# Decode states with channels on partitions, and a new order at the start and at the mixer-to-FFN seam

## The chip, the cores and the metric

One Trainium2 chip, 8 NeuronCores, one program on all of them. Each core takes one prompt sequence (2048 tokens) and 16 decode streams of 4 tokens (64 tokens, "the decode tile", tile 16). The metric is the device time of the slowest core in microseconds. Engines: PE (TensorE, matmuls and transposes), DVE (VectorE), ACT (ScalarE), POOL (GpSimd; here small copies, products and the queue of the casting weight loads), SP (SyncE; here only the queue of all other transfers).

## What is computed

One layer of a hybrid decoder in f32, weights cast to bf16 for PE:

```python
mod = silu(c) @ w_ada + b_ada            # shift1, scale1, gate1, shift2, scale2, gate2
h   = rmsnorm(x, g_pre_mix) * (1 + sc1) + sh1
v_pool, x_conv, B, C = split(h @ w_in)   # 4 x 512 channels
y_A = pool_scale * groupwise(mean_window(v_pool) - v_pool)   # windows 2, 4, 8, 16
y_B = B * dwconv3(C * x_conv)
x   = x + gt1 * rmsnorm([y_A | y_B] @ w_out, g_post_mix)
h2  = rmsnorm(x, g_pre_ffn) * (1 + sc2) + sh2
a,b = split(dwconv3(h2 @ w_up))          # 2 x 2816 channels
x   = x + gt2 * rmsnorm((silu(a) * b) @ w_down, g_post_ffn)
```

The decode streams carry state into the windows: the last 15 rows of v_pool (`state_pool`), the last 2 rows of C * x_conv (`state_conv`) and of the up projection (`state_ffn`). The new states of decode and prompt are outputs beside both y.

## The kernel before

Tokens are cut into 16 tiles of 128 and the decode tile of 64; four tiles make a chunk (0 to 3). Inside the mixer and FFN data lie with channels on partitions and tokens along the row.

Start: SP loads `cT`, the identity, `vecs` and x tiles 0 to 3 into four slots (`XT`); POOL issues eight pieces of w_ada (scale1, shift1), then `w_in_p`, `pool_w` and four `w_in_j`. A tile is squared and summed on ACT (line 540), Sqrt on ACT (542), reciprocal and product on DVE (547, 585), then its slot is free; transposed by PE (`h_tr`, 298) and scaled on the way out of PSUM (`h_ev`, 687/689, ACT or DVE).

Mixer: 16 steps `n` (chunk c = n // 4, s = n % 4). A step has `P_item(c, s)`, the pool projection of group s into bank 5, evicted by ACT (809), windows on DVE; and `V_item(c, s)`, three projections into banks 2, 3, 4 (885 to 901). In chunk 1 (`samp`) each 512-column matmul of these has a 64-column one for the decode tile beside it, so `HS`, the transposed decode tile (`samp_tr_ev`), must be there before chunk 1. The decode tile is loaded at step 2 (lines 1028 to 1031) and needs a slot. Output tiles follow five steps later: `o_tile(t)` reloads x, multiplies by w_out into banks 0 and 1 and adds the normalised result to x (`post_b1`, 933 to 941); `b2(t)` normalises for the FFN. `gate_piece` (four for gate1 at n = 4) makes the gate rows on PE (736) and DVE (741, 742) and needs the `rows` tensor. w_out follows the last w_ada piece on POOL's queue.

States before: HBM holds them row-major. `state_in` loads them with rows on partitions into `STG0` to `STG2`, PE turns them with f32 transposes, ACT copies them into `VS` [128, 4, 16, 19] and `QS` [128, 4, 16, 6]. `state_out` turns them back (two groups of four transposes, two ACT copies, 20 transfers, one of them from HBM to HBM). `ffn_state_piece` brings `state_ffn` in by six loads and 44 transposes during pairs 6 to 16 of the first FFN group; `ffn_state_out` takes it out by 44 transposes, 11 ACT copies and 22 transfers among the last down projections.

Seam: after step 15 output tiles 16 and 11 to 15, `b2` of each, the four gate2 pieces, `state_out` and `h2_all(2)` are written ahead of the FFN. FFN: group 0 (chunks 0 and 1), its down projections of tiles 0 to 7, group 1 (chunks 2, 3 and the decode tile), down projections 8 to 16. A group has 22 pairs; a pair is two chunks of 16 matmuls into one of three bank pairs (`next_pair`), evicted by ACT (1217, 1218) and two DVE products (1220, 1224), Silu on ACT (1285), product on POOL (1234). `hook0(i)` puts `b2(15)`, `h2_T(3, ..)`, the w_down loads and the state pieces behind pair i.

Order: every operation is recorded with the regions it reads and writes. Then `Sched.arrange` (184 to 234) plays all of it through with fixed costs and writes one order per engine: at each step it takes the engine that can start first and, among what could start there within 0.25 us, the operation that stands first in the program. Engines then run in that order and wait for semaphores, whatever really comes first. Transfers have no such cost of their own but one shared bus:

```python
if o.dma:
    bus = max(bus, free[e] + 1.5) + o.nbytes * DMA_US_PER_BYTE
    o.fin = bus + 0.5
```

`x` tile loads of chunk 1 depend on a PE operation: tiles 4 and 5 on the last shift1 piece (`first_x`), tiles 6 and 7 on the first `P_item` (`firsts[0]`), state and rows loads on the second (`firsts[1]`).

Of the kernel before, what the change touches and what calls it, by code (L numbers as in the profile page):

```python
# [7 lines left out]
F32 = mybir.dt.float32  # L8
# [8 lines left out]
NS = 16  # L17
# [19 lines left out]
DMA_US_PER_BYTE = 1.0 / 380e3  # L37
# [81 lines left out]
class Sched:  # L119
# [64 lines left out]
    def arrange(self):  # L184
# [11 lines left out]
        bus = 0.0  # L196
# [13 lines left out]
        while todo:  # L210
# [90 lines left out]
def build_program():  # L301
# [11 lines left out]
    stp_d = din("st_pool", [NS * PB, 512])  # L313
    stc_d = din("st_conv", [NS * 2, 512])
    stf_d = din("st_ffn", [NS * 2, 2 * DFF])
# [12 lines left out]
    npp_d = dout("npp", [PB, 512])  # L328
    ncp_d = dout("ncp", [2, 512])
    nfp_d = dout("nfp", [2, 2 * DFF])  # L330
    nps_d = dout("nps", [NS, PB, 512])
    ncs_d = dout("ncs", [NS * 2, 512])
    nfs_d = dout("nfs", [NS * 2, 2 * DFF])
# [33 lines left out]
    IDF = alloc([128, 128], F32)  # L367
# [10 lines left out]
    TMP = alloc([128, D], F32)  # L378
    h2a_off = cur[0]
# [29 lines left out]
    SMPP = alloc([128, 4, TS + PB], F32)  # L409
    SMP2 = alloc([128, 4, 34], F32)  # L410
# [4 lines left out]
    XN1 = [alloc([128, D], BF16) for _ in range(4)]  # L415
    x_end = cur[0]
# [34 lines left out]
    STF = alloc([128, NCH, 34], F32)  # L451
# [7 lines left out]
    def new_sem(name):  # L459
# [13 lines left out]
    r_vecs, r_vd, r_sc, r_rep, r_id, r_idb, r_invc, r_eps = [R(n) for n in  # L473
                                                             ("vecs", "vd", "sc", "rep", "id", "idb", "invc", "eps")]
# [82 lines left out]
    dma1("sp", IDF, ident_d, writes=[r_id])  # L557
# [66 lines left out]
    K.op("dve", lambda e: e.tensor_copy(IDB, IDF), reads=[r_id], writes=[r_idb])  # L624
# [178 lines left out]
    def P_item(c, g, samp):  # L803
# [27 lines left out]
        if c < 3:  # L831
            K.op("pool", lambda e: e.tensor_copy(V[:, 1:16], V[:, 513:528]), reads=[], writes=[rV])
        else:
            K.op("pool", lambda e: e.tensor_copy(SMPP[:, g, TS:TS + PB], V[:, 513:528]), reads=[rV], writes=[r_smpt[g]])
        if samp:
# [4 lines left out]
            def f_ev(e):  # L840
                e.activation(out=v3[:, :, PB:PB + DS], in_=ps3.rearrange("p (s r) -> p s r", r=DS), func=AF.Copy)
                return e.activation(out=SMPP[:, g, 0:TS], in_=ps3, func=AF.Copy)
            K.op("act", f_ev, reads=[r_ps[sbank]], writes=[r_vs[g], r_smpp[g]])
# [40 lines left out]
    def V_item(c, j, samp):  # L884
# [17 lines left out]
        if c < 3:  # L902
            K.op("pool", lambda e: e.tensor_copy(Q[:, 0:2], Q[:, 512:514]), reads=[], writes=[rQ])
        else:
            K.op("pool", lambda e: e.tensor_copy(SMP2[:, j, 32:34], Q[:, 512:514]), reads=[rQ], writes=[r_smp2t[j]])
        if samp:
# [14 lines left out]
            K.op("pool", lambda e: e.tensor_copy(SMP2[:, j, 0:32].rearrange("p (s r) -> p s r", r=2), q3[:, :, 4:6]),  # L921
                 reads=[r_qs[j]], writes=[r_smp2[j]])
# [86 lines left out]
    for n in range(16):  # L1009
# [4 lines left out]
        if n == 10:  # L1014
            for rr in H2Areg:
                rr.alias(r_stg + [r_rows1])
            h2_all(0)
# [4 lines left out]
        if c < 3:  # L1022
# [5 lines left out]
            if n == 2:  # L1028
                h_load(16, deps=[firsts[1]])
                h_act(16)  # L1030
                h_dve(16)
        if c < 3 and s == (3 if c == 0 else 2):
            for gi in range(4):
                h_T(c + 1, gi, misc_bank(), "act" if gi < 3 else "dve")
            if c == 0:
                samp_tr_ev(misc_bank(), XN2[0], r_xn2[0], G1T, S1T, [r_g1, r_s1], HS, 0, r_hs)
# [8 lines left out]
        if n == 1:  # L1045
            rows1_in([firsts[1]])
            state_in([firsts[1]])
# [11 lines left out]
        if n == 9:  # L1059
# [6 lines left out]
           [r_xc, r_acc, r_xcs, r_accs] + r_dbs + r_db + r_vs + r_qs + r_smpp + r_smpt + r_smp2 + r_smp2t)  # L1066
# [14 lines left out]
    def state_out():  # L1081
        K.op("pe", tr_group([PS[0:TS + PB, 5, g * 128:(g + 1) * 128] for g in range(4)],
                            [SMPP[:, g, :] for g in range(4)], IDF), reads=r_smpp + r_smpt + [r_id], writes=[r_ps[5]])
        K.op("act", lambda e: e.activation(out=TT_[0][0:TS + PB, 0:512], in_=PS[0:TS + PB, 5, :], func=AF.Copy),
             reads=[r_ps[5]], writes=[r_tt[0]])
        K.op("pe", tr_group([PS[0:34, 5, j * 128:(j + 1) * 128] for j in range(4)],
                            [SMP2[:, j, :] for j in range(4)], IDF), reads=r_smp2 + r_smp2t + [r_id], writes=[r_ps[5]])
        K.op("act", lambda e: e.activation(out=TT_[1][0:34, 0:512], in_=PS[0:34, 5, :], func=AF.Copy),
             reads=[r_ps[5]], writes=[r_tt[1]])
        out_ops.append(K.dma("sp", lambda e: [e.dma_start(out=nps_d[s, PB - DS:PB, :], in_=TT_[0][s * DS:(s + 1) * DS, 0:512])  # L1090
                                              for s in range(NS)] + [e.dma_start(out=npp_d, in_=TT_[0][TS:TS + PB, 0:512])],
                             next_misc(), NS + 1, reads=[r_tt[0]]))
# [45 lines left out]
    STGF = USB[0].rearrange("p a b c -> p (a b c)")  # L1138
    STG_F = [STGF[:, 0:384], None]

# [7 lines left out]

    STA = TMP
    r_sta = r_tmp  # L1150
    s_sta = new_sem("sta")

    def ffn_state_piece(n, bank):
        q0, q1 = n * 8, min(NCH, n * 8 + 8)
        nq = q1 - q0
        dma1("sp", STA[0:32, 0:nq * 128], stf_d[:, q0 * 128:q1 * 128], writes=[r_sta], sem=s_sta)
        K.op("pe", tr_group([PS[:, bank, q * 32:(q + 1) * 32] for q in range(nq)],
                            [STA[0:32, q * 128:(q + 1) * 128] for q in range(nq)], IDF[0:32, 0:32]),
             reads=[r_sta, r_id], writes=[r_ps[bank]])
        K.op("act", lambda e: e.activation(  # L1160
# [272 lines left out]
```

How the kernel before makes its waits and increments, by code:

```python
    def emit(self, eng, e):  # L248
        waited = {}
        for o in self.ops[eng]:
            need = {}
            for d in o.deps:
                s, v = d.sig
                if need.get(s, 0) < v:
                    need[s] = v
            for s, v in need.items():
                if waited.get(s, 0) < v:
                    e.wait_ge(s.h, v)
                    waited[s] = v
            if o.fn is None:
                continue
            r = o.fn(e)
            if o.dma:
                assert len(r) == o.n, (len(r), o.n)
                for i in r:
                    i.then_inc(o.sem.h, 16)
            elif o.need:
                r.then_inc(o.sig[0].h, 1)
```

## Time and profile before

| | |
|---|---|
| median of 3 runs | 798.16 us (797.77 to 799.29) |
| profiled execution | 796.71 us, span of its slowest core 795.2 us |
| spans of the 8 cores | 788.0 to 795.2 us, clock 0.972 to 0.984 |
| PE busy | 717.5 us, 90% |
| DVE, ACT, POOL busy | 488.9, 337.4, 206.1 us |
| DMA packets | 27211, of them 4741 under 512 B |

The page is of the slowest core. Busy time is the sum of an engine's instructions in a stretch; a stretch in which PE's busy time equals its length is bound by PE. "Idle before" and the name behind the arrow say what released an instruction that had to wait.

### The profile page before, as it was taken

How to read it: one execution, taken by the hardware profiler on the slowest of the kernel's cores; microseconds unless marked ns; L12 is line 12 of the kernel's file. 1: busy time of each engine (PE TensorE's matmuls, PEld its weight loads, DVE VectorE, ACT ScalarE, POOL GpSimd, SP SyncE). 2: the span in 40 equal slices, each digit the busy share in tenths (PEclk: the TensorE clock that was granted, in tenths of full speed). 3: DMA queues.
4: the chain of work that ended last, by engine and by line, in shares of the span. 5: the costliest groups of instructions: out<-in, count | busy, mean ns of one | idle time of the engine just before them, and what ended most of it. 6: DMA issues, size and time to landing. Idle time of an engine off the chain costs nothing.

```text
span 795.2 us, 12501 instructions; the slowest of 8 cores (788.0 to 795.2 us)
## 1 busy us (share of the span) xinstructions
PE 717.5 (90%) x4204; PEld 351.4 (44%) x4204; DVE 488.9 (61%) x660; ACT 337.4 (42%) x607; POOL 206.1 (26%) x266
## 2 busy tenths in 40 slices
PE   0269498998999999999999999999999999999995
PEld 0224254444444554444444444444444444444442
DVE  1246278686687787777767732227888888832222
ACT  1226235644565466655444421114544445422221
POOL 4001010011010001543444420003667667530000
PEclk9979599999899999999999999999999999999999
DMA  8999977319942496488874523234344343003321
GB/s 152 200 191 218 200 186 187 106 54 193 214 150 93 115 239 201 80 166 155 152 141 80 79 54 131 104 110 108 56 83 75 63 85 67 1 13 139 116 78 40
DMA packets 27211, 96.88 MB, mean 122 GB/s; under 512 B 4741, under 2 KB 4997, under 8 KB 26236
## 3 DMA queue, kind: packets, MB, share of 16 engines
q0 software_dynamic: 11904, 47.85, 35.7%
q1 hardware_dynamic: 15244, 48.23, 18.3%
q8 instruction: 34, 0.56, 0.3%
q14 instruction: 29, 0.24, 0.1%
HBM read 125.61 MB, written 18.66 MB: 181 GB/s over the span
## 4 chain that ended last, share of the span: by engine, by line
PE 80%; DMA 11%; DVE 3%; ACT 3%; issue 2%; POOL 1%; DVEq 0%; another core or an unknown queue 0%; ACTq 0%; POOLq 0%; SPq 0%
PE ps L785 50%; PE ps L290 20%; PE ps L281 6%; DMA arena<-w_in_p 5%; DMA arena<-x 3%; DMA arena<-w_ada 2%; PE ps L298 2%; PE ps L736 1%; ACT arena L687 1%; DVE arena L935 1%; ACT arena L540 1%; POOL arena L521 1%; DVE arena L1220 0%; DVE arena L1224 0%; DVE arena L939 0%
## 5 line engine op out<-in xcount | busy, mean ns | idle before, releaser
L785 PE MATMUL ps<-arena 128*128 128x512 bf16 (+1 forms) x2400 | 442.6, 346 | 12.4 <-DMA arena<-w_in_p 6.1
L785 PEld LDWEIGHTS ps<-arena 128*128 128x128 bf16 x2400 | 201.9, 99 | 242.1 <-issue 24.5
L290 PE MATMUL ps<-arena 128*128 128x512 bf16 (+1 forms) x748 | 162.9, 379 | 0.0
L1220 DVE SCALAR_TENSOR_TENSOR arena<-ps,arena 128x1023 f32<-128x1023 f32 x88 | 112.7, 1281 | 53.8 <-ACT arena L1218 53.5
L1234 POOL TENSOR_TENSOR arena<-arena 128x1024 bf16<-128x1024 f32 x44 | 103.6, 2354 | 86.7 <-DVE arena L1224 61.5
L1224 DVE SCALAR_TENSOR_TENSOR arena<-ps,arena 128x1022 f32<-128x1022 f32 x88 | 112.8, 1281 | 9.2
L290 PEld LDWEIGHTS ps<-arena 128*128 128x128 bf16 (+1 forms) x748 | 73.6, 99 | 86.7 <-issue 0.4
L540 ACT ACTIVATE arena<-ps 128x1024 f32<-128x1024 f32 (+1 forms) x34 | 34.8, 1023 | 155.6 <-PE ps L290 128.5
L547 DVE RECIPROCAL arena<-arena 128x1 f32<-128x1 f32 (+1 forms) x68 | 10.8, 158 | 143.8 <-ACT arena L542 143.7
L1218 ACT ACTIVATE arena<-ps,arena 128x1024 f32<-128x1024 f32 x88 | 97.5, 1109 | 0.1
L1217 ACT ACTIVATE arena<-ps 128x2 f32<-128x2 f32 x88 | 15.1, 172 | 129.8 <-PE ps L785 117.3
L281 PE MATMUL ps<-arena 128*128 128x512 bf16 (+1 forms) x288 | 68.3, 385 | 0.7 <-DVE arena L935 0.7
L298 PE MATMUL ps<-arena 128*128 128x128 bf16 (+4 forms) x380 | 34.3, 242 | 37.1 <-DVE arena L721 19.3
L521 POOL DMA_DIRECT2D arena<-w_up x44 | 25.8, 585 | 144.8 <-PE ps L785 114.7
L540 ACT ACTIVATE arena<-arena 128x1024 bf16<-128x1024 f32 (+1 forms) x34 | 35.9, 1055 | 35.3 <-DMA arena<-x 31.3
L1285 ACT ACTIVATE arena<-arena 128x1024 f32<-128x1024 f32 x44 | 46.5, 1057 | 8.9 <-DVE arena L1228 8.8
L298 PEld LDWEIGHTS ps<-arena 128*128 128x128 bf16 (+4 forms) x380 | 28.7, 113 | 48.0 <-issue 43.6
L939 DVE TENSOR_TENSOR arena<-arena 128x1024 f32<-128x1024 f32 (+1 forms) x34 | 41.6, 1225 | 9.1 <-DMA arena<-x 4.6
L935 DVE SCALAR_TENSOR_TENSOR arena<-ps,arena 128x1024 f32<-128x1024 f32 (+1 forms) x34 | 43.6, 1283 | 5.5 <-DVE arena L547 2.9
L687 ACT ACTIVATE arena<-ps,arena 128x512 bf16<-128x512 bf16 x48 | 33.6, 780 | 22.2 <-PE ps L298 13.6
L281 PEld LDWEIGHTS ps<-arena 128*128 128x128 bf16 (+1 forms) x288 | 27.6, 99 | 33.7 <-issue 4.1
L821 DVE TENSOR_TENSOR arena<-arena 128x512 f32<-128x512 f32 (+6 forms) x40 | 27.7, 693 | 11.4 <-ACT arena L809 9.5
(89 smaller groups left out, 381.8 us busy)
## 6 DMA issues: line engine op xcount, KB each, us to landing
arena<-w_up POOLq DMA_DIRECT2D x44, 512.0 KB, 6.2
arena<-x SPq DMA_DIRECT2D x32, 512.0 KB, 8.0
y<-arena SPq DMA_DIRECT2D x32, 512.0 KB, 2.7
arena<-w_ada POOLq DMA_DIRECT2D x24, 512.0 KB, 16.1
arena<-y SPq DMA_DIRECT2D x16, 512.0 KB, 3.7
arena<-w_down POOLq DMA_DIRECT2D x3, 1536.0 KB, 15.2
arena<-w_in_j POOLq DMA_DIRECT2D x4, 768.0 KB, 54.6
arena<-rows SPq DMA_DIRECT2D x4, 512.0 KB, 15.8
```

Source lines behind the costliest of these rows:

```text
L281: inst = e.matmul(out_ap, lhs_list[i], rhs_list[i], start=(i == 0), stop=(i == n - 1))
L290: inst = e.matmul(out_ap, lhs_list[i], rhs_list[i], start=(first and i == 0), stop=(last and i == n - 1))
L298: inst = e.transpose(o, i, ident)
L540: K.op("act", lambda e: e.activation(out=junk, in_=src_ap, func=AF.Square, accum_out=STAT[0:rows, k_ss, t:t + 1]), reads=src_regs, writes= ...
L785: inst = e.matmul(o_, l_, r_, start=st, stop=sp_)
L935: K.op("dve", lambda e: e.scalar_tensor_tensor(TMP[0:rows, :], psv, STAT[0:rows, k_rs, t:t + 1], GTt[0:rows, :], ALU.mult, ALU.mult), read ...
L939: lambda e: e.tensor_tensor(XT[xi][0:rows, :], TMP[0:rows, :], XT[xi][0:rows, :], ALU.add),
L1218: return e.activation(out=tv, in_=psv, func=AF.Copy, scale=fw_of(2, c))
L1220: K.op("dve", lambda e: e.scalar_tensor_tensor(tv[:, 1:1024], psv[:, 0:1023], fw_of(1, c), tv[:, 1:1024], ALU.mult, ALU.add), reads=rp + [ ...
L1224: K.op("dve", lambda e: e.scalar_tensor_tensor(tv[:, 2:1024], psv[:, 0:1022], fw_of(0, c), tv[:, 2:1024], ALU.mult, ALU.add), reads=rp + [ ...
L1234: K.op("pool", lambda e: e.tensor_tensor(GT_[:, i, 0:1024], ta, tb, ALU.mult), reads=[rTa, rTb], writes=[r_g[i]])
L1285: K.op("act", lambda e, ta=ta: e.activation(out=ta, in_=ta, func=AF.Silu), reads=[rTa], writes=[rTa])
```

## The change

Host code now lays the states out as [128 partitions, channel block, stream, row] and pads the rows of the first two to 19 and 6. The kernel loads them straight into `VS`, `QS` and `STF`, and stores them straight from there; all state transposes, their staging tiles and ACT copies go.

```diff
-DMA_US_PER_BYTE = 1.0 / 380e3
+DMA_US_PER_BYTE = 1.0 / 340e3
@@ arrange
-                bus = max(bus, free[e] + 1.5) + o.nbytes * DMA_US_PER_BYTE
-                o.fin = bus + 0.5
+                move = o.nbytes * DMA_US_PER_BYTE
+                if e == "pool":
+                    bus = max(bus, free[e] + 1.5) + move
+                    o.fin = bus + 0.5
+                else:
+                    side = max(side, free[e] + 1.5) + 1.7 * move
+                    bus += move
+                    o.fin = side + 0.5
@@ start: the decode tile after tiles 0 to 3
+    h_load(16)
+    h_act(16)
+    h_dve(16)
...
+    samp_tr_ev(2, XN2[0], r_xn2[0], G1T, S1T, [r_g1, r_s1], HS, 0, r_hs)
@@ state_in
+        dma1("sp", VS.rearrange("p a b c -> p (a b c)"), stp_d, writes=r_vs, deps=deps)
+        dma1("sp", QS.rearrange("p a b c -> p (a b c)"), stc_d, writes=r_qs, deps=deps)
@@ P_item, V_item, chunk 3 (c == 3) and samp
-            K.op("pool", lambda e: e.tensor_copy(SMPP[:, g, TS:TS + PB], V[:, 513:528]), ...
+            out_ops.append(dma1("sp", npp_d[:, g, :], V[:, 513:528], reads=[rV]))
-                return e.activation(out=SMPP[:, g, 0:TS], in_=ps3, func=AF.Copy)
-            K.op("pool", lambda e: e.tensor_copy(SMP2[:, j, 32:34], Q[:, 512:514]), ...
+            out_ops.append(dma1("sp", ncp_d[:, j, :], Q[:, 512:514], reads=[rQ]))
-            K.op("pool", lambda e: e.tensor_copy(SMP2[:, j, 0:32]. ...
@@ steps
-            if n == 2:
-                h_load(16, deps=[firsts[1]])
-                h_act(16)
-                h_dve(16)
         if n == 1:
-            rows1_in([firsts[1]])
-            state_in([firsts[1]])
+            state_in([firsts[0]])
+        if n == 2:
+            rows1_in([firsts[2]])
@@ state_out
+        out_ops.append(K.dma("sp", lambda e: [e.dma_start(out=nps_d[:, g, :, :], in_=VS[:, g, :, DS:DS + PB]) for g in range(4)],
+                             next_misc(), 4, reads=r_vs))
+        out_ops.append(K.dma("sp", lambda e: [e.dma_start(out=ncs_d[:, j, :, :], in_=QS[:, j, :, 4:6]) for j in range(4)],
+                             next_misc(), 4, reads=r_qs))
@@ seam, new order
+    o_tile(16, 2); b2(10); o_tile(11, 0); gate2[0](); ffn_load(0, 0); b2(16); gate2[1](); ffn_load(0, 1)
+    b2(11); o_tile(12, 2); gate2[2](); ffn_load(0, 2); state_out(); h2_all(2); gate2[3](); ffn_load(0, 3)
+    samp_tr_ev(6, XNS, r_xns, G2T, S2T, [r_g2, r_s2], H2B, 1024, r_h2s)
@@ hook0(i)
-        if i == 0:
-            b2(15)
-        if i in (1, 2, 3, 4):
-            h2_T(3, i - 1, 6 + i % 2, "act")
-        if i == 4:
-            p1y()
-        if i in (5, 8, 11, 14):
-            load_wdn((i - 5) // 3)
-        if 6 <= i < 18 and i % 2 == 0:
-            ffn_state_piece((i - 6) // 2, 6 + (i // 2) % 2)
+        if i < 3:
+            o_tile(13 + i, next_pair())
+            b2(12 + i)
+        if i == 3:
+            b2(15)
+        if i in (4, 5, 6, 7):
+            h2_T(3, i - 4, 6 + i % 2, "act")
+        if i == 7:
+            p1y()
+            dma1("sp", flat(STF), stf_d, writes=[r_stf])
+        if i in (8, 10, 12, 14):
+            load_wdn((i - 8) // 2)
@@ after FFN group 1; all ffn_state_out go
+    out_ops.append(dma1("sp", nfs_d, flat(STF), reads=[r_stf]))
+    out_ops.append(dma1("sp", nfp_d, flat(STFP), reads=r_stfp))
```

(The new order of the seam stands here with several calls in a line.) The identity moves into a part of `TMP`, which is free after the start; the last two prompt rows of the FFN state get a tile of their own, `STFP`.

## Rows read from the trace of the kernel before

**Rows 1.** The stage table, the whole span in stretches (columns in its second line).
```profile
core 6: us, PE busy (x) PEld busy (x) DVE busy (x) ACT busy (x) POOL busy (x), PEclk, DMA share, GB/s
0.00:47.00 47.00, 7.32 (x160) 6.92 (x160) 10.03 (x60) 11.45 (x19) 8.99 (x28) 0.93 0.97 174
...
71.00:99.00 28.00, 14.94 (x83) 8.56 (x82) 11.51 (x23) 11.28 (x20) 2.52 (x6) 0.70 1.02 208
99.00:138.00 39.00, 34.18 (x254) 19.21 (x252) 30.14 (x64) 19.46 (x44) 3.63 (x11) 0.96 0.76 192
138.00:180.00 42.00, 40.53 (x305) 20.56 (x303) 31.37 (x60) 23.50 (x52) 2.97 (x10) 0.96 0.24 78
...
299.00:323.00 24.00, 23.09 (x123) 10.96 (x124) 18.55 (x22) 16.50 (x28) 4.64 (x5) 1.00 0.66 181
323.00:458.30 135.30, 135.30 (x660) 62.41 (x658) 98.31 (x78) 66.32 (x104) 59.51 (x43) 1.00 0.68 122
...
715.00:787.00 72.00, 71.86 (x355) 34.90 (x352) 18.72 (x21) 14.51 (x33) 0.00 (x0) 1.00 0.29 102
```

**Rows 2.** Timeline of PE, 47 to 106 us.
```profile
start us, us, engine line op out<-in xcount [idle before <-releaser]
...
47.28 3.57 PE L785 MATMUL ps<-arena 128*128 128x512 bf16 x8 [6.05 <-DMA arena<-w_in_p]
...
77.30 1.06 PE L298 MATMUL ps<-arena 128*128 128x128 bf16 x16
87.61 1.03 PE L298 MATMUL ps<-arena 120*128 120x120 f32 x4 [9.26 <-DMA arena<-st_pool]
92.45 3.31 PE L298 MATMUL ps<-arena 120*128 120x120 f32 x24 [3.80 <-DMA arena<-st_pool]
...
99.10 4.00 PE L736 MATMUL ps<-arena 128*128 128x256 bf16 x32
...
105.18 9.67 PE L785 MATMUL ps<-arena 128*128 128x512 bf16 x64 [1.74 <-DVE arena L700]
```

**Rows 3.** Timeline of the queue SP, the issues of x (columns as before).
```profile
41.48 0.33 SPq L521 DMA_DIRECT2D arena<-x  x1
...
51.09 0.85 SPq L521 DMA_DIRECT2D arena<-x  x2
...
70.99 6.52 SPq L521 DMA_DIRECT2D arena<-x  x4
...
179.18 11.30 SPq L521 DMA_DIRECT2D arena<-x  x3
```

**Rows 4.** DMA issues 41.48, 51.6, 70.99, 179.18: queue, count, KB, us to landing.
```profile
arena<-x SPq DMA_DIRECT2D x1, 512.0 KB, 13.6
...
arena<-x SPq DMA_DIRECT2D x1, 512.0 KB, 22.0
...
arena<-x SPq DMA_DIRECT2D x1, 256.0 KB, 27.2
...
arena<-x SPq DMA_DIRECT2D x1, 512.0 KB, 15.6
```

**Rows 5.** Timeline of ACT, 19 and 67 us.
```profile
19.12 1.28 ACT L542 ACT_TABLE_LOAD   x1
...
67.48 1.05 ACT L540 ACTIVATE arena<-arena 128x1024 bf16<-128x1024 f32 x1
```

**Rows 6.** The chain that ended last (start us, us, what).
```profile
5.92 41.23 DMA arena<-w_in_p
...
269.86 0.44 PE ps L298 x4
...
322.42 13.97 PE ps L785 x64
...
350.65 0.61 PE ps L298 x8
...
715.47 0.87 PE ps L298 x8
```

**Rows 7.** DMA, 2 to 3 us: packets, MB, share; then cT's issue.
```profile
q1 hardware_dynamic: 734, 0.05, 53.5%
...
arena<-cT SPq DMA_DIRECT2D x1, 72.0 KB, 3.7
```

More of the change, by code:

```diff
@@ L195, in arrange @@
         ready = {}
-        bus = 0.0
+        bus = side = 0.0
         def admit(o):
@@ L312, in build_program @@
     cT_d = din("cT", [D, 18])
-    stp_d = din("st_pool", [NS * PB, 512])
-    stc_d = din("st_conv", [NS * 2, 512])
-    stf_d = din("st_ffn", [NS * 2, 2 * DFF])
+    stp_d = din("st_pool", [128, 4 * NS * (PB + DS)])
+    stc_d = din("st_conv", [128, 4 * NS * (2 + DS)])
+    stf_d = din("st_ffn", [128, NCH * 32])
     wada_d = din("w_ada", [24 * 128, KC * 256])
@@ L327, in build_program @@
     y_d = dout("y", [NTOK, D])
[L328 to L333, printed above, removed]
+    npp_d = dout("npp", [128, 4, PB])
+    ncp_d = dout("ncp", [128, 4, 2])
+    nfp_d = dout("nfp", [128, NCH * 2])
+    nps_d = dout("nps", [128, 4, NS, PB])
+    ncs_d = dout("ncs", [128, 4, NS, 2])
+    nfs_d = dout("nfs", [128, NCH * 32])
     ARENA_BYTES = 207 * 1024
@@ L1147, in load_wdn @@
         dma1("pool", flat(WDN[:, i0:i1, :]), wdn_d[:, i0 * D:i1 * D], writes=[r_wdnq[q]], sem=s_wdnq[q])
[L1149 to L1160, printed above, removed]
-            out=STF[:, q0:q1, 0:32], in_=PS[:, bank, 0:nq * 32].rearrange("p (q r) -> p q r", q=nq),
-            func=AF.Copy), reads=[r_ps[bank]], writes=[r_stf])
     def fw_of(kk, c):
@@ L1363, in build_program @@
             down_b(t - 1)
-            for _ in range(2):
-                if so:
-                    ffn_state_out(so.pop(0))
     return finish()
@@ L1414 @@
         m["cT"] = np.ascontiguousarray(np.concatenate([c_prompt[i:i + 1], c_sample[sl], np.zeros((1, D), np.float32)], axis=0).T)
-        m["st_pool"] = np.ascontiguousarray(state_pool[sl].reshape(NS * PB, 512))
-        m["st_conv"] = np.ascontiguousarray(state_conv[sl].reshape(NS * 2, 512))
-        m["st_ffn"] = np.ascontiguousarray(state_ffn[sl].reshape(NS * 2, 2 * DFF))
+        m["st_pool"] = cmaj(state_pool[sl], DS)
+        m["st_conv"] = cmaj(state_conv[sl], DS)
+        m["st_ffn"] = cmaj(state_ffn[sl], 0)
         in_maps.append(m)
@@ L1425 @@
     y_s = np.concatenate([rs[i]["y"][T:NTOK].reshape(NS, DS, D) for i in range(NCORES)], axis=0)
-    npp = np.stack([rs[i]["npp"] for i in range(NCORES)], axis=0)[None]
-    ncp = np.stack([rs[i]["ncp"] for i in range(NCORES)], axis=0)[None]
-    nfp = np.stack([rs[i]["nfp"] for i in range(NCORES)], axis=0)[:, :, inv][None]
-    nps = np.concatenate([rs[i]["nps"] for i in range(NCORES)], axis=0)[None]
-    ncs = np.concatenate([rs[i]["ncs"].reshape(NS, 2, 512) for i in range(NCORES)], axis=0)[None]
-    nfs = np.concatenate([rs[i]["nfs"].reshape(NS, 2, 2 * DFF) for i in range(NCORES)], axis=0)[:, :, inv][None]
+    npp = np.stack([rmaj(rs[i]["npp"]) for i in range(NCORES)], axis=0)[None]
+    ncp = np.stack([rmaj(rs[i]["ncp"]) for i in range(NCORES)], axis=0)[None]
+    nfp = np.stack([rmaj(rs[i]["nfp"].reshape(128, NCH, 2)) for i in range(NCORES)], axis=0)[:, :, inv][None]
+    nps = np.concatenate([rmaj(rs[i]["nps"]).reshape(NS, PB, 512) for i in range(NCORES)], axis=0)[None]
+    ncs = np.concatenate([rmaj(rs[i]["ncs"]).reshape(NS, 2, 512) for i in range(NCORES)], axis=0)[None]
+    nfs = np.concatenate([rmaj(rs[i]["nfs"].reshape(128, NCH, 32)).reshape(NS, 2, 2 * DFF) for i in range(NCORES)], axis=0)[:, :, inv][None]
     return tuple(np.ascontiguousarray(a.astype(np.float32)) for a in (y_p, y_s, npp, ncp, nfp, nps, ncs, nfs))
```

116 lines of the change are left out of this document (27 added, 89 removed).

## The prediction

> **What bounds the kernel now.** I read the stage table first [rows 1]. TensorE (PE) is the bound wherever its busy time equals the stretch: 135.30 of 135.30 us at 323 to 458 and 71.86 of 72.00 at 715 to 787. It is not in three places: the start (7.32 of 47 us), 71 to 99 (14.94 of 28, granted clock 0.70, the lower of its two levels for part of it) and 99 to 138 (34.18 of 39). The missing time of the last two is 13.1 + 4.8 = 17.9 us. In 71 to 99 the DMA share is 1.02, in 138 to 180 it is 0.24.
>
> The timeline of PE [rows 2] shows who is waited for: after 16 transposes at 77.30 nothing until 87.61, where the state transposes wait 9.26 us and then 3.80 us for st_pool; chunk 1 of the prompt begins at 105.18, behind the decode tile's two DVE steps. The queue SP [rows 3] explains it: tiles 4 and 5 go out at 41.5 and 42, tiles 6 and 7 at 51.1, the decode tile at 70.99 and lands 27.2 us later [rows 4], at 98.2. Tile 4 lands 13.6 us after issue (55.1), tile 7 22.0 us after 51.6 (73.6): three tiles of 512 KB in 18.5 us, 6.2 us each. ScalarE (ACT) touches tile 4 only at 67.48 [rows 5], 12.4 us after landing: the planner had put it late. The first projection waits for w_in_p, landed at 47.15 [rows 6].
>
> **The change part by part.** The sum is against the profiled execution, 796.71 us, its span of 795.2 and 1.5 around it; the median shown, 798.16, is 1.45 above it.
>
> *Tail.* 44 f32 transposes go: five pieces of 0.87 us and one of 0.44, the first at 715.47 [rows 6], 4.8 us in a stretch where PE never waits [rows 1]. Their 11 ACT copies and 22 small stores were hidden. Two SP stores replace them. The last tile's chain after 787 stays. Gain 4.8.
>
> *FFN states in.* 44 transposes between pairs 6 and 16 go: five times 0.61 (the one at 350.65 stands for them) and one of 0.36 [rows 6], 3.4 us, PE saturated [rows 1]. One 720 KB load replaces six; it goes out after pair 7 and is needed in the second FFN group, over 100 us later: nothing. Gain 3.4.
>
> *Mixer states out, PE part.* Two groups like the one at 269.86, 0.44 each [rows 6]: 0.9. The dropped small copies of ACT and GpSimd had cover: nothing.
>
> *Start, to 47 us.* The decode tile's 256 KB now go through before w_ada's last piece and w_in_p. 10 MB of f32 weights and 2 MB of x pass in some 45 us up to there [rows 6], so 0.26 MB more delay w_in_p 1.0 us. The tile's normalising, its transposes and two DVE steps lie in the wait for w_in_p. Bounds 0 (another order) and 2.3 us (all of it alone). Loss 1.0, counted in the next part.
>
> *47 to 138 us.* The decode tile (98.2) and the state transposes (92.4) stop being waits. Late next is tile 7. Its place gets worse: the state loads now depend on the same projection as tiles 6 and 7 but come first in program order, so SP issues st_pool and st_conv (819 KB, padded; 544 KB before) ahead of both. At 6.2 us per 512 KB that is 9.6 us: tile 6 lands at 67.4 + 1.0 + 9.6 = 78, tile 7 at 84. Tiles 8 and 9, released by tiles 4 and 5, then also stand ahead of the rows, which the gates need: rows land near 106, where they used to be in ahead of the decode tile's 98.2.
> And the new planner separates SP's transfers from GpSimd's. By its constants (I use them for order only) tile 4 arrives just ahead of the first projection's end, tile 5 right behind it, tiles 6 and 7 during V items 1 and 2. Engines run in this written order, so ACT, which evicts PE's banks, would stand at tile 4 until 56, tile 5 until 63, tile 6 until 78, tile 7 until 84, and PE behind it for want of banks 5 and 2 to 4. Following the order: P(0,0)'s bank, full near 51 [rows 2], is free at 58, V(0,1) ends near 88, then V(0,2), V(0,3), the 32 transposes and the last P item, some 9 us of PE left of them, end near 97. Chunk 1 then starts at 97, not 105.2: 8.2 gained. The two gate pieces at 99.10 [rows 2], 4.0 us, lay in the old wait and now cost their time; of the 4.8 us idle in 99 to 138 I take 3 back, because tile 10 no longer waits for the decode tile's slot. 8.2 - 4.0 + 3 is 7, the 1.0 of the start already in it. Bounds: +17.9, all idle time of both stretches; -5, if the gates' DVE steps stand until 106 and the ACT waits chain. I take +7, nearest to the landing rows.
>
> *Mixer states out, the stores.* These are the part to fear. nps takes 15 of 19 floats per stream (60-byte runs), 4 x 128 x 16 = 8192 runs; ncs takes 2 of 6 floats (8 bytes), 8192 more. npp and ncp add 1024. The trace has small runs once: cT, 1024 runs of 72 bytes. In the microsecond 2 to 3 there were 734 packets of 68 bytes at a DMA share of 53.5% [rows 7]: 1372 a microsecond at full share, 12 us for 16,384. cT took 3.7 us from issue to landing [rows 7], latency included: 16 times that is 59 us. Those are loads; a store of 8 bytes has no row, so both ends stand. They go out when chunk 1's last P and V items are evicted (168 in the old timeline) and SP's queue is first in, first out. The next load that is pressed is the one at 179.18, which already lands only after 15.6 us [rows 3, 4], 11 us later. The wait is thus X - 11: 1 to 48. I take X = 15, between the ends but by the packet row, as the DMA share there is low (0.24 [rows 1]): loss 4. Whoever waits: DVE's residual add, behind it every DVE eviction, then PE.
> The Trainium skill ("DMA: Bandwidth & Descriptors", Rules for kernel authors) says a strided last dimension gives one descriptor per element, and its Specifications say that under 512 bytes there is a read-modify-write. The first, for runs, agrees with the 68-byte packets of [rows 7]; the second no row here shows for stores, and it speaks for the upper end.
>
> *Last output tiles among FFN pairs 0 to 3.* PE's work is the same; a pair is half of 13.97 us [rows 6]. What could be won is what PE lacks at 299 to 323, 0.9 us [rows 1]. What is added is that Silu and Sqrt alternate on ACT: eight more table loads (two for each of four pairs) of 1.28 us, as at 19.12 [rows 5], 10.3 us on ACT, in a stretch where ACT was busy 16.50 of 24 us. Over some 31 us that makes 21.3 + 10.3: ACT about full, and it evicts the banks. Bounds: 0.9 won, 10.3 lost; I take 2 lost, since part of that ACT work (h2_T of chunk 3) moves to later pairs.
> The row at 19.12 ends where the next instruction begins (20.41) and starts 0.07 us after the one before. The Trainium skill ("ScalarE: Activation LUTs", What ACT_TABLE_LOAD costs) adds a drain of 1.38 us, 2.66 in all. The trace doesn't agree, and it decides. By the page the loads would cost ACT 21.3 us and this part about 10 lost.
>
> **Sum:** -4.8 - 3.4 - 0.9 - 7 + 4 + 2 = -10.1. 786.6 against the profiled execution, 788.0 against the median.
>
> **Rivals.**
> *A, the starting stages open fully.* If the planner sets ACT's work on tiles 4 to 7 behind the evictions as before, chunk 1 starts as soon as tile 7 is in, near 90, and the wait of the stores is hidden. For it: ACT was late, not early, at 67.48 [rows 5]. Against: the new side bus in the planner is made of 2.6 us per tile where the queue needs 6.2. -9.1 - 15 + 1 + 1 = -22: 776.
> *B, nothing gained before 138.* The ACT waits and the late rows eat the decode tile's gain: -9.1 + 0 + 4 + 2 = -3: 795. For it: DMA share 1.02 [rows 1], so loads only trade places. Against: 13 us of PE wait had named causes that go.
> *C, slower: the small stores block SP's queue.* One mechanism, between 168 and 230 in the old timeline: at X = 59 the loads of tiles for output and chunk 3 come 48 us late instead of 4, DVE stands, PE too: 788 + 44 = 832. It decides from X = 25 on, 25 ns a run on each engine, twice what [rows 7] shows by packets. For it: 8-byte stores are smaller than anything in the trace. Against: DMA is nearly idle there.
> *D, the alternation costs its whole ACT time:* 8 us more, 796. It is inside the range.
>
> **How the numbers follow.** Forecast 788: 0.45. A 0.22, B with D 0.20, C 0.13. About 0.2% (1.6 us) is what the measurement can tell. Faster: all of the forecast and A, and 0.16 of B and D: 0.83. Same: 0.04 of B and D and the edge of C, 0.01. Slower: 0.12 of C. The range reaches down to A less 2 (774) and up into mild C, X near 30 (804); outside are the worst of C (0.10) and the best of A (0.06).
>
> **What would show it.** Right: no f32 transposes among the down projections, which then follow each other without gaps; PE between 323 and 458 shorter by 3.4; chunk 1 (first matmuls with 64 columns) at 92 to 100; ACT's L540 waits for x longer than before; eight more ACT_TABLE_LOADs; thousands more packets under 512 bytes and an x load behind them landing 10 us or more after issue. Wrong: PE waiting at all for st_pool; chunk 1 at 105 or later; DVE's residual add waiting tens of microseconds near 180; a wait for banks over 5 us in FFN pairs 0 to 3.

## The result: 933.9 us, 16% slower, and where the 136 us are

The changed kernel takes 933.92 us in the median of four runs (921.07 to 943.36), the kernel before 798.72 beside it. The ratio is 1.160 with a 95% interval of 1.145 to 1.175; two of the four runs were disturbed, and the ratio is of the other two, 921.07 and 930.99. The forecast was 788, range 774 to 804: wrong in size and in sign. Rival C named the mechanism (the small stores block SP's queue) and priced it at 832 with the queue held for 59 us; it is held for up to 157.

The page of the changed kernel: span 941.8 us (core 6), with PE busy 75% of it, 90% before. It is the longest execution of the four (943.36 us), so the lengths read from it are upper ones.

```profile
span 941.8 us, 12098 instructions; the slowest of 8 cores (902.2 to 941.8 us)
...
PE 706.2 (75%) x4021; PEld 341.4 (36%) x4096; DVE 491.6 (52%) x660; ACT 337.2 (36%) x589; POOL 201.7 (21%) x254
...
PE   0366959600007029998889999999999999999996
...
PEclk9987999955558559999999999999999999999999
DMA  9999962999959996237474997423343343402321
GB/s 164 186 207 239 162 132 91 24 1 1 16 11 47 75 169 183 92 112 170 113 160 102 173 168 145 69 88 112 112 113 68 68 72 67 88 1 77 116 76 56
DMA packets 44173, 97.11 MB, mean 103 GB/s; under 512 B 22160, under 2 KB 22544, under 8 KB 43216
```

PE does less than before in all (706.2 against 717.5 us) and the span is 147 us longer. The digits (40 slices of 23.5 us) show the place: in the eighth to fourteenth slice, 165 to 330 us, PE is near 0 in most, the DMA engines are mostly at 9, and they move 24, 1, 1, 16, 11, 47 and 75 GB/s. Packets under 512 bytes went from 4741 to 22160. The timeline of the queue SP names what runs there (start us, us, what; it answers to the last row of [rows 3]):

```profile
168.55 37.34 SPq L1062 DMA_DIRECT2D ncs<-arena  x4
206.10 26.05 SPq L524 DMA_DIRECT2D arena<-x  x1
232.24 60.32 SPq L1060 DMA_DIRECT2D nps<-arena  x4
292.66 32.82 SPq L524 DMA_DIRECT2D y<-arena  x1
```

`ncs` is 8192 runs of 8 bytes, `nps` 8192 of 60. From 168.55 SP issues only these, one load of x squeezed between them, and one y store, which is not through until 325.5: 157 us for 16,384 runs, 9.6 ns a run over the 16 engines, 153 ns on each. Core 6 is the slowest here; the same stretch of SP's queue takes 126 to 149 us on the other seven cores, 7.7 to 9.1 ns a run. All eight cores store at the same time (the groups begin between 164 and 172 us), and no run has one core alone. The DMA view of two stretches shows about the same rate for both lengths of run:

```profile
q1 hardware_dynamic: 2676, 0.02, 192.5%
...
q1 hardware_dynamic: 6123, 0.85, 98.0%
```

The first row is 180 to 206 us, 2676 packets of 8 bytes in 26 us, 103 a microsecond; the second is 232 to 290 us, 6123 packets (5995 of them small) in 58 us, 106 a microsecond (103 of small ones). [Rows 7] had 734 in one microsecond for small loads. The rate isn't low from the start: at 170 to 175 us, behind the first issue, 2138 small packets went through, 428 a microsecond. So 9.6 ns is the mean of a group that slows down within some microseconds; what fills up there no run shows.

Who pays is in the waits (engine, line, what it waited for, total us, times, longest):

```profile
ACT arena L543 <- DMA arena<-x: 206.4, 12, 108.1
...
PE ps L772 <- ACT arena L880: 109.9, 2, 105.2
...
DVE arena L922 <- DMA arena<-x: 42.4, 1, 42.4
```

ACT stands at an x tile, and PE stands behind ACT, which evicts its banks (L880). DVE's residual add (L922), which the prediction named as the first to wait, waits once, 42.4 us, and later.

The stage table of the changed kernel, to be read against [rows 1]:

```profile
core 6: us, PE busy (x) PEld busy (x) DVE busy (x) ACT busy (x) POOL busy (x), PEclk, DMA share, GB/s
47.00:71.00 24.00, 14.79 (x54) 5.68 (x53) 8.07 (x17) 5.18 (x10) 1.65 (x5) 0.86 1.01 207
71.00:99.00 28.00, 20.20 (x97) 9.04 (x99) 12.15 (x22) 12.56 (x22) 2.68 (x7) 0.82 0.90 219
99.00:138.00 39.00, 31.88 (x233) 18.08 (x235) 25.76 (x55) 12.38 (x29) 3.18 (x9) 0.96 0.83 152
...
169.00:326.00 157.00, 31.21 (x203) 14.41 (x205) 19.77 (x40) 12.87 (x27) 3.46 (x9) 0.60 1.34 23
...
500.00:620.00 120.00, 119.42 (x558) 54.78 (x568) 84.98 (x67) 58.62 (x88) 52.85 (x42) 1.00 0.73 129
700.00:845.00 145.00, 144.01 (x927) 70.58 (x945) 122.06 (x118) 72.52 (x120) 95.88 (x116) 1.00 0.36 63
845.00:933.00 88.00, 87.63 (x408) 40.27 (x411) 27.41 (x31) 15.75 (x31) 8.57 (x9) 1.00 0.23 84
```

In 169 to 326 PE is busy 31.2 of 157 us, at a granted clock of 0.60, 23 GB/s through engines shown as full. From 500 on PE is saturated, as before; nothing of the loss is there.

One forecast was close, within 1.2 us, and helps below: ACT stands at x tiles 4 to 7 in written order (timeline of ACT; forecast 56, 63, 78, 84 us):

```profile
56.02 1.06 ACT L543 ACTIVATE arena<-arena 128x1024 bf16<-128x1024 f32 x1 [10.17 <-DMA arena<-x]
62.03 1.06 ACT L543 ACTIVATE arena<-arena 128x1024 bf16<-128x1024 f32 x1 [3.99 <-DMA arena<-x]
77.88 1.06 ACT L543 ACTIVATE arena<-arena 128x1024 bf16<-128x1024 f32 x1 [9.57 <-DMA arena<-x]
82.85 1.06 ACT L543 ACTIVATE arena<-arena 128x1024 bf16<-128x1024 f32 x1 [2.95 <-DMA arena<-x]
...
283.28 1.06 ACT L543 ACTIVATE arena<-arena 128x1024 bf16<-128x1024 f32 x1 [108.09 <-DMA arena<-x]
```

### The profile page after: what moved, and what is told of

Its sections match the earlier page's. It is cut to its first block, busy times and chain, and to the rows that moved or that the text cites. A ratio compares the mean times of both kernels' runs of the same rounds, so it can differ in the third digit from the quotient of the medians.

```text
span 941.8 us, 12098 instructions; the slowest of 8 cores (902.2 to 941.8 us)
## 1 busy us (share of the span) xinstructions
PE 706.2 (75%) x4021; PEld 341.4 (36%) x4096; DVE 491.6 (52%) x660; ACT 337.2 (36%) x589; POOL 201.7 (21%) x254
## 4 chain that ended last, share of the span: by engine, by line
PE 61%; SPq 17%; DMA 10%; DVE 5%; issue 3%; ACT 3%; DVEq 0%; ACTq 0%; POOLq 0%
PE ps L772 37%; PE ps L296 17%; DMA arena<-x 9%; SPq L524 7%; SPq L1060 6%; PE ps L287 4%; SPq L1062 4%; PE ps L304 1%; ACT arena L688 1%; PE ps L737 1%; ACT arena L543 1%; DMA arena<-w_up 1%; DVE arena L918 1%; DVE arena L1166 1%; DVE arena L1162 1%
## 5 line engine op out<-in xcount | busy, mean ns | idle before, releaser
L922 DVE TENSOR_TENSOR arena<-arena 128x1024 f32<-128x1024 f32 (+1 forms) x34 | 43.2, 1271 | 46.3 <-DMA arena<-x 42.4
L524 POOL DMA_DIRECT2D arena<-w_ada x24 | 12.9, 545 | 242.9 <-PE ps L715 168.0
L722 DVE TENSOR_TENSOR arena<-ps,arena 128x34 f32<-128x34 f32 x16 | 3.1, 192 | 113.1 <-PE ps L715 112.3
L715 PE MATMUL ps<-arena 128*128 128x18 bf16 x256 | 8.6, 174 | 55.8 <-ACT arena L864 38.7
L688 ACT ACTIVATE arena<-ps,arena 128x512 bf16<-128x512 bf16 x48 | 33.6, 775 | 17.7 <-PE ps L304 10.4
```

What stands on the lines that cost most here:

```text
L524: return K.dma(eng, lambda e: [e.dma_start(out=out_ap, in_=in_ap)], sem if sem is not None else next_misc(), 1, reads=reads, writes=writes ...
```

## The experiments

**Are the small stores the cause, and how much?** e1 is the changed kernel with whole-row stores of `VS` and `QS`: one run per partition, the host cuts the needed columns out.

```diff
-            nps_d[:, g, :, :] <- VS[:, g, :, DS:DS + PB]   (4 transfers, 60-byte runs)
-            ncs_d[:, j, :, :] <- QS[:, j, :, 4:6]          (4 transfers, 8-byte runs)
+        out_ops.append(dma1("sp", nps_d, VS.rearrange("p a b c -> p (a b c)"), reads=r_vs))
+        out_ops.append(dma1("sp", ncs_d, QS.rearrange("p a b c -> p (a b c)"), reads=r_qs))
```

> The changed kernel with one edit: the new mixer states are stored as whole rows of VS and QS (4864 and 1536 bytes a partition, padding included) instead of 16,384 runs of 60 and 8 bytes; the host takes the wanted columns. Theory R (the small runs hold SP's queue): the wait between 169 and 326 us goes, time 786 to 800 us, since chunk 1 started at 101 instead of 105 and the state transposes are gone. Theory P (the new planner's order and the seam lose the time): it stays above 900 us. Theory H (half each): near 860.

Measured 809.19 us (ratio 1.0143, 1.0121 to 1.0166). So 933.9 - 809.2 = 124.7 us are the two groups of stores (116 by the ratios), and 11 us of loss remain that are something else; they put e1 above the 800 us that theory R allowed.

e2 makes only `ncs` whole rows; the 8192 runs of 60 bytes stay.

> The changed kernel with only ncs stored as whole rows; nps keeps its 8192 runs of 60 bytes. If a run costs the same whatever its size (9.6 ns over all engines in the changed kernel, 157 us for 16,384): 8192 runs are 79 us, less some 11 us of slack, 855 to 870 us. If the 8-byte runs are the dear ones: under 820. If the 60-byte runs are: over 900. Theory P: over 900 as well.

Measured 855.63 (1.0723): 46 us over e1 for half of the runs. SP's timeline of e2:

```profile
170.46 58.39 SPq L1060 DMA_DIRECT2D nps<-arena  x4
228.94 10.07 SPq L524 DMA_DIRECT2D y<-arena  x1
```

68.5 us for 8192 runs, 8.4 ns each (49 to 63 us on the other cores): the price goes by the run. Between the profiled executions these 68.5 us of queue cost 45.7 us (854.37 - 808.65), and the 157 us of the changed kernel cost 134.7 (943.36 - 808.65). So some 22 us are hidden in both, twice the 11 that the forecast took for the slack of the tiles already loaded. It is used only once, and half the stores cost less than half the loss.

e3 (one time, 811.06) is e1 that also copies the same 16,384 runs from `VS` and `QS` to two other SBUF tiles that nothing reads; `VS` and `QS` are stored as whole rows, as in e1. e13 is e1 with 16,384 loads of 60 and 8 bytes from HBM instead, e14 is e1 with 16,384 further stores to HBM, each at its own 512-byte boundary. e4 is the kernel before with 16,384 packed stores into a scratch tensor. The core of each:

```diff
e3  + VC[:, g, :, :] <- VS[:, g, :, DS:DS + PB];  QC[:, j, :, :] <- QS[:, j, :, 4:6]
e13 + VC[:, g, :, :] <- stp4[:, g, :, DS:DS + PB];  QC[:, j, :, :] <- stc4[:, j, :, 4:6]
e14 + scr1 = dram [128, 4, NS, 128];  scr1[:, g, :, 0:PB] <- VS[:, g, :, DS:DS + PB]; the same for QS
e4  + scr1 = dram [128, 4, NS, PB];   scr1[:, g, :, :] <- VS[:, g, :, DS:DS + PB]; the same for QS
```

> Whole-row stores as in the first run of this group, and beside them the same 16,384 runs of 60 and 8 bytes copied from VS and QS into a free place of SBUF, at the same point of SP's queue; nothing reads the copy. If a run costs by itself, whatever it is written to: 157 us of queue again, 920 to 935 us. If it is the small write to HBM that is slow: the copy takes 12 to 40 us and the time is 790 to 820 us. Theory P: above 900 without a block in SP's queue.

> Whole-row stores (809 us) and the mirror of the stores: 16,384 runs of 60 and 8 bytes loaded from HBM (columns of the state inputs) into a free place of SBUF that nothing reads. If small accesses of HBM are slow both ways: 900 us or more. If only small writes to HBM are: like the copy inside SBUF, 809 to 825 us.

> Whole-row stores and 16,384 small stores of 60 and 8 bytes to a scratch tensor in HBM in which each run starts at its own 512-byte boundary. If neighbours that share a line hold each other up: 810 to 840 us. If each small write costs by itself (9.6 ns over all engines): 930 to 960 us.

> The kernel before, with eight more stores: the same 16,384 runs of 60 and 8 bytes from VS and QS into a scratch tensor in HBM, once chunk 1 is done; everything else is the kernel before. Theory R: SP's queue is held for about 150 us from 168 on and the time is 930 to 945 us. Theory P: the queue takes them beside its other work, 800 to 815 us.

| 16,384 runs of 60 and 8 bytes | added to | SP in the two groups | SP's queue held | time added |
|---|---|---|---|---|
| SBUF to SBUF (e3, 811.06) | e1 | 12 us | 16 us | 1.9 us |
| HBM to SBUF (e13, 816.65) | e1 | 32 us | 38 us | 7.4 us |
| SBUF to HBM, one run per 512 bytes (e14, 851.4) | e1 | 36 us | 61 us | 42 us |
| SBUF to HBM, packed (changed kernel, 933.92) | e1 | 98 us | 157 us | 124.7 us |
| SBUF to HBM, packed (e4, 959.58) | before | 111 us | 186 us | 161.7 us |

"Held" runs from the first issue of the two groups to the end of the last issue, of whatever kind, ahead of the two or three x loads in a row with which the queue goes on. Both columns of SP are from the slowest core of the profiled execution; in e14 the eight cores have 57 to 70 us, in e3 16 to 29.

The timelines of SP behind the two columns, e3, e13, e14 and e4 in this order:

```profile
169.39 4.46 SPq L999 DMA_DIRECT2D arena<-arena  x4
...
175.69 7.79 SPq L997 DMA_DIRECT2D arena<-arena  x4
```

```profile
170.91 6.53 SPq L1002 DMA_DIRECT2D arena<-st_conv  x4
...
179.68 25.03 SPq L1000 DMA_DIRECT2D arena<-st_pool  x4
```

```profile
171.65 16.76 SPq L1064 DMA_DIRECT2D scr<-arena  x4
188.45 16.19 SPq L526 DMA_DIRECT2D ncs<-arena  x1
...
205.29 19.11 SPq L1062 DMA_DIRECT2D scr<-arena  x4
224.44 6.63 SPq L526 DMA_DIRECT2D nps<-arena  x1
```

```profile
163.59 48.09 SPq L1086 DMA_DIRECT2D scr<-arena  x4
211.89 62.85 SPq L523 DMA_DIRECT2D arena<-x  x1
274.83 62.49 SPq L1084 DMA_DIRECT2D scr<-arena  x4
337.42 12.44 SPq L523 DMA_DIRECT2D y<-arena  x1
```

The cause is neither the count of runs nor their shortness by themselves (e3, e13) but small writes to HBM, packed ones above all, and they do it in a kernel that has no other part of the change (e4). The runs cost more in e4, above the 945 us that its theory R allowed; they come on top of all of the old kernel's own stores there, but that this is the reason was not shown. e14 came out between its two theories (810 to 840 and 930 to 960): small writes cost 42 us even when each has 512 bytes to itself, and packed about three times that.

The Trainium skill ("DMA: Bandwidth & Descriptors", Why small descriptors are slow) says that transfers from SBUF to SBUF do not suffer from small runs as those with HBM do; e3 agrees, 16 us of held queue against 157. Its Specifications put a read-modify-write on everything under 512 bytes. e14's runs are under that too and hold the queue for 61 us, against 157 for the packed ones, so that rule alone does not tell the two apart. What the packed ones pay beyond, some 96 us, may come with runs that share a block of HBM and wait for one another there. That is a likely reading and was not shown: e14 also gives each run another starting address (packed runs start every 60 or 8 bytes) and spreads them over 8 MB, no run tries a spacing between 8 and 512 bytes, and none has a single core storing.

**What of the rest of the change is good?** e5, e6 and e7 are e1 with one part undone: the planner's transfer model, the seam, the start.

```diff
e5  -    side = max(side, free[e] + 1.5) + 1.7 * move          (SP; POOL on bus), 340e3
    +    bus = max(bus, free[e] + 1.5) + o.nbytes * DMA_US_PER_BYTE          380e3
e6  -    b2(10) and h2 work between o_tile(11..12); o_tile(13..15) inside hook0(0..2)
    +    o_tile(11..15), gate2 and b2(10..14) ahead of the FFN, as before
e7  -    h_load(16); h_act(16); h_dve(16) after tiles 0 to 3; states on firsts[0]
    +    the same at n == 2; rows and states on firsts[1], as before
```

> Whole-row stores (809 us) with the planner's transfer model of the kernel before (one bus, 380e3). Theory O (the new model writes ACT's work on tiles 4 to 7 ahead of PE's evictions, and later x loads ahead of need; that is the rest of the loss): 788 to 796. Rival S (the seam with its alternation loses it): 805 to 811. Rival T (the start's new order of loads loses it): 803 to 811.

> Whole-row stores with the old seam: output tiles 13 to 15 ahead of the FFN, the transposes of chunk 3 behind pairs 1 to 4. Rival S: 798 to 802. Theory O or rival T: 806 to 811; the forecast had put 2 us on this part.

> Whole-row stores with the old start: the decode tile at step 2, rows and states behind the second projection, the new planner kept. Rival T: 796 to 802. Theory O: 806 to 815, as the decode tile is a wait again and ACT still stands at tiles 4 to 7.

Measured 796.48 (0.9987, 0.9976 to 0.9998), 805.47 (1.0094) and 807.97 (1.0127) against 809.19. The planner's model costs e1 12.7 us, the seam 3.7, the start 1.2. That is 17.6; the layout pays 9.1 back (e8, below), which leaves 8.5 of the 11.3 that e1 lies above the kernel before. The other 2.8 belong to no single part. e5 ends just above the range of theory O (788 to 796), e6 just below that of theory O or T.

e8 is the other way round: the kernel before with the layout alone, whole-row stores. e10 adds the seam to e8, e11 the decode tile at the start (into `TMP`, so that it takes no slot).

> The kernel before with the state layout alone (whole-row stores; planner, start and seam of before). The 9.1 us of PE transposes that were counted, and some of the 13 us in which PE waited for st_pool: 780 to 789 us by every theory; 788 or more if the transposes were partly hidden.

> The state layout with the new seam, planner and start of the kernel before. The whole-row kernel with the old seam was 3.7 us faster than with the new one; if the seam costs the same everywhere: 791 to 794 us. If it was the new planner's order at the seam: 787 to 790.

> The state layout on the kernel before (788.7 us), and the decode tile loaded behind tiles 0 to 3 into TMP, so that it takes no slot of XT, and normalised there; states and rows stay behind tiles 6 and 7. In the states-only kernel PE waited 12.79 us for this tile and 2.22 for its DVE steps, with chunk 1 at 104.35. Theory W (the tile is the only late thing there): chunk 1 at 90 to 93, time 774 to 780 us. Rival L (loads only trade places, DMA share 1.0): st_pool or tile 8 is late next, time 785 to 789.

e8: 788.72 us, ratio 0.9896 (0.9864 to 0.9928), 9.1 us under the 797.85 beside it. That is the sum of the counted transposes, 4.8 + 3.4 + 0.9. The 13 us of waits for st_pool brought nothing: in e8 PE waits 12.79 us for the decode tile in their place, and chunk 1 begins at 104.35. e10: 794.77 (0.9959), so the seam costs 6.0 us by itself (5.0 by the ratios). e11: 792.37 (0.9930), above both of its theories and 3.7 us over e8 (2.7 by the ratios), although chunk 1 begins at 88.73 instead of 105.18 [rows 2]. The timelines of PE and of ACT in e11 say why:

```profile
88.73 6.04 PE L776 MATMUL ps<-arena 128*128 128x512 bf16 x48
...
107.75 3.46 PE L776 MATMUL ps<-arena 128*128 128x512 bf16 x16 [12.97 <-DVE arena L544]
```

```profile
70.92 1.05 ACT L537 ACTIVATE arena<-arena 128x1024 bf16<-128x1024 f32 x1
...
103.27 1.06 ACT L537 ACTIVATE arena<-arena 128x1024 bf16<-128x1024 f32 x1 [13.59 <-DMA arena<-x]
```

ACT reaches tile 4 at 70.92, some 15 us after it can be there (e18, with the same first loads, takes it at 54.92); its slot is free late, tile 8's load goes out at 74.56 (SP), and ACT then stands 13.59 us at tile 8 and PE behind it. e12 writes the state loads ahead of the rows load in e11.

> As e11 (the old shared-bus planner, decode tile at the start) with the state loads written ahead of the rows load. Theory 1 (written order of ACT at tile 8): nothing of it changes unless tile 8's load moves; 790 to 794, PE's wait near 108 stays 10 to 13 us. Rival (the order of the loads decides, rows ahead of states make tile 8 late): the wait falls by the 3 to 5 us of one load, 786 to 789.

Measured 793.5 (0.9943), inside the first theory's range, though PE's longest wait there falls to 8.19 us, below the 10 to 13 expected. The time doesn't follow it: the order of those two loads is not the cause.

**Does a planner with the measured rate give the time back?** The changed kernel's model moves an x tile in 2.6 us (1.7 x 512 KB / 340 KB per us); the landings of [rows 4] are 6.2 us apart. e15 is e11 with the separate SP model and that rate. e17 uses it only while the planner's own clock is under 100 us, e18 under 75, and the old shared bus afterwards.

```diff
e15  side = max(side, free[e] + 1.5) + 4.0 * move          (340e3)
e17  if e == "pool" or free[e] > 100.0:  bus = max(bus, free[e] + 1.5) + move;  o.fin = bus + 0.5
     else:  side = max(side, free[e] + 1.5) + 4.5 * move;  bus = bus + move;  o.fin = side + 0.5     (380e3)
e18  the same with 75.0
```

> The layout, whole-row stores and the decode tile at the start (as e11), now with the planner's separate reckoning of SP's transfers, its rate set to 4.0 x (6.2 us for 512 KB at 340 KB/us, as the landings show) in place of 1.7 x. Theory 1 (ACT stands in written order at x loads that the planner believed early, and that is the 13 us wait of e11 and the 12.7 us that the new model cost): with the measured rate ACT's waits of 13.59 and 4.75 us for tiles 8 and 9 go, PE's 12.97 us wait near 108 falls below 4, and the time is 776 to 784. Rival (the loads are simply late, whatever the order of ACT): the wait only moves to another line and the time is 789 to 795.

> As e15, but the planner uses the separate slow reckoning of SP's transfers (4.5 x 512 KB / 380 KB per us = 6.2 us) only while its own time is under 100 us, and the old shared bus afterwards. If e15's loss lies after 138 us, in orders made for loads that are quick there (DMA share 0.34 to 0.65), the start keeps e15's PE busy 47.3 of 52 us at 47 to 99, the later stages those of e11, and the time is 780 to 788. Rival: the order at the start by itself pushes work behind 99 us that nothing absorbs there; 789 to 800.

> The same with 75 us in place of 100. Tile 8's load (issued at 74.6 us in e11) is then reckoned by the old bus and ACT stands at it as in e11: by the theory that ACT's written order makes the 13 us wait, PE's wait near 108 us is back in part (5 to 13 us) and the time is 2 to 8 us above e17. Rival: no difference between the two (within 2 us).

e15: 816.92 (1.0233), far above both expectations, though the waits went nearly as expected: ACT waits 1.02 and 4.13 us near 101 and 109, and PE's longest wait near 110 is 2.13 us. e17: 784.76 (0.9841, 0.9814 to 0.9869). e18: 783.66 (0.9822, 0.9799 to 0.9846), the best kernel of this case, 14 us under the kernel before by its ratio. The stage tables, first e15, then e18, then e11:

```profile
47.00:99.00 52.00, 47.34 (x275) 23.24 (x276) 31.91 (x60) 21.70 (x40) 6.23 (x18) 0.93 1.03 210
99.00:138.00 39.00, 29.44 (x158) 14.44 (x157) 22.56 (x47) 15.45 (x32) 1.50 (x4) 0.78 0.86 206
...
180.00:240.00 60.00, 47.69 (x307) 23.11 (x306) 38.91 (x63) 30.73 (x58) 3.75 (x10) 0.91 0.65 151
...
299.00:345.00 46.00, 33.04 (x161) 14.40 (x158) 23.96 (x31) 25.32 (x43) 4.00 (x4) 0.89 0.40 126
```

```profile
47.00:99.00 52.00, 46.85 (x276) 23.42 (x276) 33.54 (x64) 22.26 (x40) 6.15 (x18) 0.93 1.03 211
99.00:138.00 39.00, 30.19 (x204) 15.32 (x203) 24.71 (x50) 20.64 (x43) 1.48 (x4) 0.91 0.84 205
...
180.00:240.00 60.00, 55.69 (x364) 27.71 (x363) 43.35 (x70) 30.74 (x59) 3.27 (x10) 0.94 0.76 183
```

```profile
47.00:99.00 52.00, 42.64 (x242) 20.83 (x240) 25.77 (x48) 18.11 (x32) 6.57 (x15) 0.93 1.02 207
99.00:138.00 39.00, 24.00 (x137) 11.60 (x138) 23.90 (x48) 14.50 (x32) 1.92 (x6) 0.76 0.73 166
```

Up to 138 us e15 and e18 are alike, PE 76.8 and 77.0 us busy against 66.6 in e11: the right rate at the start is worth 10.4 us of PE's time by 138, and 8.7 us at the end (792.37 to 783.66, by the ratios 8.6). In e18 ACT takes tile 4 at 54.92, SP issues tile 8 at 57.77, and chunk 1 begins at 87.13. e15 then loses 7.7 us at 180 to 240 and 10.4 at 299 to 345 (33.04 against 43.39 in e11), where loads are quicker and the planner treats them as slow; e17 and e18, which drop the rate there, do not (55.45 and 44.91 us in e17). e18 was expected 2 to 8 us above e17 and is equal to it within 1.1 us. That does not test what it was meant to: tile 8's load now goes out at 57.77, ahead of the 75 us, so most likely it has the slow rate in both. What is shown is that with ACT's work on tile 4 written early, tile 8's load goes out 17 us sooner and the 13 us wait is gone.

## Why the prediction was wrong, step by step

| term | forecast | by medians | by ratios | from |
|---|---|---|---|---|
| states without transposes (tail, FFN in, mixer out) | -9.1 | -9.1 | -8.3 | e8 against before |
| seam | +2 | +6.0 | +5.0 | e10 - e8 |
| start and planner | -7 | +14.4 | +14.7 | e1 - e10 |
| small stores | +4 | +124.7 | +116 | changed kernel - e1 |
| sum | -10.1 | +136 | +127 | |

The ratio column is each difference of ratios times 798 us.

**The step that failed is "Mixer states out, the stores".** Its mechanism was right in the main: the runs fill SP's first-in, first-out queue when chunk 1's last items are evicted (168 forecast, 168.55 seen), and x loads come late; it is ACT that stands first, for 108 us, and not DVE's residual add. Its price was not: X, the queue's time, was bounded by 12 and 59 us and set to 15; it is 157 (126 to 149 on the other cores), and the loss of 4 us is 124.7. The slack of 11 us was too small as well, but next to X that is little: it is about 22. Both ends came from rows of small loads [rows 7], with the remark that a store had no row, but then "both ends stand" as though they bounded it. For loads they do: e13's 16,384 small loads take SP 32 us and hold its queue for 38. A row of the other direction was no bound at all. The rule of the Trainium skill ("DMA: Bandwidth & Descriptors", Specifications) on transfers under 512 bytes, cited as speaking for the upper end, was a reason to open the range above it. The argument against C, that DMA is nearly idle there, says nothing about a queue that is limited by its own transfers. C's chance of 0.13 was too low and its 832 was only the top of the same wrong bounds.

**47 to 138 us, a second miss of 21 us.** The 21 us are all of e1 - e10, +14.4, against the -7 of this part. The ends of ACT's waits were right to 1.2 us each, and chunk 1 began at 101.14 in the timeline of PE, not 97 (before: 105.18 [rows 2]):

```profile
101.14 5.04 PE L772 MATMUL ps<-arena 128*128 128x512 bf16 x39
```

What was missed is that the same belief (2.6 us for a tile that takes 6.2) orders all later stages too. Between e5 and e1, which differ only in the planner's model, PE's busy time falls from 71.36 to 63.80 us at 47 to 138, and by 4.3 and 5.8 us in 138 to 169 and 169 to 326 (some of it is made up later, 12.7 arrive in the time), where ACT in e1 stands at x once more (11.08 us at 209). The forecast stopped at 138. It also took 8.2 us for an earlier chunk 1; e11 shows that an earlier chunk 1 (88.73) brought nothing while ACT stands at the tiles behind it.

**The seam** was forecast +2 within -0.9 to +10.3. The eight more table loads are there (before 3 + 2 + 1, after 7 + 6 + 1, each 1.28 us), and PE in e10 is busy 19.63 of 22 us at 323 to 345, a stretch it fills before [rows 1]. Taking 2 discounted work that moves to later pairs; the cost is about half of the loads' 10.3 us. That the table loads make it was not shown: no run has the new seam without them, and of the 5 to 6 us only these 2.4 were placed in a stretch.

**The states** were right within the measurement (e8's interval is 5.7 to 10.9 us): each term was PE time in a stretch without a wait, counted by instruction; no run tells the three terms apart. The tail's down projections now follow each other without transposes between them, and PE waits for st_pool nowhere.

## What to carry to other kernels

A resource with no row of its own kind has no bound: a small load's price says nothing of a small store's, so an edit that puts thousands of short runs into an HBM tensor is worth leaving until one is measured, or is made harmless by storing whole rows and cutting them on the host, which costs no device time beyond the padding. Transposes counted in a saturated stretch were worth their time here (9.1 us counted, 9.1 measured, between 5.7 and 10.9). A planner's transfer rate is part of the kernel: too fast at a crowded start makes engines stand in written order at loads not yet there, too slow where the queue is quick loses more; take the rate of each stage from its landings.

## What the runs showed of the hardware

- With eight cores storing at once, packed stores of 8 and 60 bytes to HBM cost about the same, 9.6 ns a run over 16 engines (153 ns on one) on the slowest core and 7.7 on the quickest, 23 GB/s and less through engines that show as full; the same runs hold SP's queue for 16 us from SBUF to SBUF instead of 157, for 38 as loads from HBM, for 61 as stores 512 bytes apart.
- It is mostly their own queue that they block: an x load issued behind the first group, at 206.10 us, took 77.1 us to land (15.6 in [rows 4]), while a w_ada load on POOL's queue at 232 to 290 us took 15.2 and the five of 169 to 326 us 20.6 in the median. The kernel before has 15.4 for eight w_ada loads at 170 to 200 us, which come close behind one another; so POOL's queue runs on, but this does not show that it runs undisturbed.
- PE's granted clock over the stall was 0.60 in the mean, so mostly the lower of its two levels (1.2 of 2.4 GHz), with PE busy 31.2 of 157 us.
